# Two-block transformer kernel on one core: the division of the sparse heads' probabilities moved from VectorE to ScalarE, one tile ahead

## The reference, cut to what matters

```
s = jnp.einsum('bqhd,bqkhd->bhqk', qb, k_sel) * (Dh ** -0.5)
s = jnp.where(valid[:, None], s, NEG)
p = jax.nn.softmax(s, axis=-1)          # exp, row sum, division
o = jnp.einsum('bhqk,bqkhd->bqhd', p, v_sel)
```

## Time and profile before

| | before |
|---|---|
| median of 3 runs | 1163.38 us (1163.32 to 1163.65) |
| the profiled execution | 1163.7 us |
| its span, first to last instruction | 1161.6 us |
| PE busy | 1143.0 us (98% of the span) |
| DVE busy | 598.2 us (51%) |
| ACT busy | 288.1 us (25%) |
| POOL busy | 712.4 us (61%) |
| granted TensorE clock, mean | 0.999 |
| sparse tiles, 709 to 777 us: PE / DVE / ACT busy | 65.66 / 49.99 / 41.57 of 68.00 us |

### The profile page before, as it was taken

The page is one execution under the profiler, slowest core; times in us unless marked ns, Lnnn a source line. Parts: engine busy times, 40 slices in busy tenths (PEclk is TensorE's granted clock), DMA queues, the critical chain, the costliest instruction groups (busy, mean ns, idle before and its releaser), DMA issues.

```text
span 1161.6 us, 15385 instructions
## 1 busy us (share of the span) xinstructions
PE 1143.0 (98%) x5319; PEld 923.0 (79%) x5319; DVE 598.2 (51%) x985; ACT 288.1 (25%) x577; POOL 712.4 (61%) x435
## 2 busy tenths in 40 slices
PE   7999999999999999999999998999999999999997
PEld 5888788888888888888777776777888888888886
DVE  4999674540014544448789778846554000455022
ACT  5134362210002111110211346645421000211001
POOL 7879948656666666657456333225876666666662
PEclk9999999999999999999999999999999999999999
DMA  6321224222222222234332221112233223223521
GB/s 243 127 86 60 77 69 143 92 97 103 90 99 99 90 101 99 90 104 133 114 123 92 90 78 57 31 56 73 91 108 108 91 91 109 91 90 108 145 73 73
DMA packets 51394, 113.12 MB, mean 97 GB/s; under 512 B 21520, under 2 KB 22160, under 8 KB 51344
## 3 DMA queue, kind: packets, MB, share of 16 engines
q1 hardware_dynamic: 31200, 105.40, 26.9%
q10 hardware_dynamic: 20144, 7.05, 2.6%
HBM read 102.99 MB, written 2.10 MB: 90 GB/s over the span
## 4 chain that ended last, share of the span: by engine, by line
PE 92%; DVE 6%; issue 1%; ACT 1%; DMA 0%; DVEq 0%; SPq 0%; ACTq 0%
PE bank L561 20%; PE bank L563 20%; PE bank L562 20%; PE bank L1096 5%; PE bank L1098 5%; PE bank L1097 5%; DVE bank L1593 2%; PE bank L941 2%; PE bank L594 1%; PE bank L593 1%; PE bank L595 1%; PE bank L627 1%; PE bank L619 1%; PE bank L620 1%; PE bank L955 1%
## 5 line engine op out<-in xcount | busy, mean ns | idle before, releaser
L426 POOL TENSOR_TENSOR wl<-raw,wh 128x1024 fp32r<-128x1024 f32 x188 | 453.1, 2410 | 15.7
L423 POOL TENSOR_SCALAR wh<-raw 128x1024 fp32r<-128x1024 f32 x188 | 203.4, 1082 | 388.9 <-PE bank L563 231.1
L561 PE MATMUL bank<-xh,wh 128*128 128x512 f32 (+1 forms) x776 | 306.1, 394 | 0.4 <-ACT va L1325 0.4
L562 PE MATMUL bank<-xl,wh 128*128 128x512 f32 (+1 forms) x776 | 300.6, 387 | 0.0
L563 PE MATMUL bank<-xh,wl 128*128 128x512 f32 (+1 forms) x776 | 300.6, 387 | 0.0
L561 PEld LDWEIGHTS bank<-xh,wh 128*128 128x128 f32 x776 | 145.7, 188 | 44.6 <-issue 16.5
L1807 DVE TENSOR_TENSOR ul<-tmb,uh 128x512 f32 x64 | 124.7, 1948 | 90.1 <-ACT uh L1268 90.1
L563 PEld LDWEIGHTS bank<-xh,wl 128*128 128x128 f32 x776 | 145.7, 188 | 29.5
L562 PEld LDWEIGHTS bank<-xl,wh 128*128 128x128 f32 x776 | 145.8, 188 | 27.7 <-issue 0.2
L1267 ACT ACTIVATE tmb<-tmp 128x512 f32<-128x512 f32 x64 | 40.5, 633 | 413.3 <-DVE tmp L1804 413.3
L561 PE MATMUL bank<-uh,wh 128*128 128x512 f32 x288 | 112.6, 391 | 0.0
(11 more groups left out here) (278 smaller groups left out, 1382.0 us busy)
## 6 DMA issues: line engine op xcount, KB each, us to landing
raw<-wstream SPq DMA_DIRECT2D x188, 512.0 KB, 3.2
x<-xT SPq DMA_DIRECT2D x8, 256.0 KB, 4.9
x4r<-x4b ACTq DMA_DIRECT2D x16, 128.0 KB, 2.7
out<-x4r SPq DMA_DIRECT2D x8, 256.0 KB, 2.3
qd<-ropey ACTq DMA_DIRECT2D x16, 64.0 KB, 2.1
kd<-ropey ACTq DMA_DIRECT2D x16, 64.0 KB, 2.0
qa<-ropey SPq DMA_DIRECT2D x16, 64.0 KB, 2.0
ka<-ropey SPq DMA_DIRECT2D x16, 64.0 KB, 2.0
```

The lines of the kernel that those rows point to most:

```text
L423: nc.gpsimd.tensor_scalar(wh[c][:], raw[c][:], 1.0, 1.0, ALU.mult, ALU.mult).then_inc(high_ready, 1)
L426: nc.gpsimd.tensor_tensor(wl[c][:], raw[c][:], wh[c][:].bitcast(F32), ALU.subtract).then_inc(split_ready, 1)
L561: mm(out, wh_, mh, start=start, stop=False)
L562: mm(out, wh_, ml, start=False, stop=False)
```

## The change

`normalise(n)` of a sparse tile keeps only one reciprocal, over the two row sums of the tile together (128x2), and raises a new semaphore `sum_inverted`. It waits for both exponentials of the tile. The two multiplications go to ACT: a new function `divide(n)` waits for `sum_inverted` and scales both halves of the tile in place with `ACT.Copy`. ACT calls it in its step n for tile n + 1, ahead of `exp(n + 2)`, and after `keep_turned(n)`, the roots and the high part of a differential head. Differential tiles stay as they are.

```diff
             def divide(n):
+
+                diff, h, tb = tile_of(n)
+                N = (tb + 1) * P
+                slot = 2 * (n % 3)
+                f = 16 + 4 * (n % 3)
+                act.wait_ge(sum_inverted, n - DIFF_TILES + 1)
+                for e in range(2):
+                    p = probs[slot + e][:, 0:N]
+                    A(p, p, ACT.Copy, scale=soft[:, f + e:f + e + 1]).then_inc(probs_ready, 1)
...
                     A(xh[:, 4 + h], kept[h][:] if h < 2 else NB[:], ACT.Copy).then_inc(xh_ready, 1)
+                if DIFF_TILES <= n + 1 < TILES:
+                    divide(n + 1)
                 if n + 2 < TILES:
                     exp(n + 2)
...
                 else:
-                    for e in range(2):
-                        p = probs[slot + e][:, 0:N]
-                        dve.wait_ge(exp_done, 2 * n + e + 1)
-                        link(V.reciprocal(soft[:, f + e:f + e + 1], soft[:, 8 + slot + e:9 + slot + e]))
-                        V.tensor_scalar(p, p, soft[:, f + e:f + e + 1], None, ALU.mult).then_inc(probs_ready, 1)
+                    dve.wait_ge(exp_done, 2 * n + 2)
+                    V.reciprocal(soft[:, f:f + 2], soft[:, 8 + slot:10 + slot]).then_inc(sum_inverted, 1)
```

More of the change, by code:

```diff
@@ L319, in build @@
             sem("pT_ready"), sem("pv_done"), sem("o_kept"))
-        lam_exp, eps_scaled = sem("lam_exp"), sem("eps_scaled")
+        lam_exp, eps_scaled, sum_inverted = sem("lam_exp"), sem("eps_scaled"), sem("sum_inverted")
         ym_gained, y_scaled, x4_ready, x4_kept = (
@@ L1364, in keep_turned, with divide @@
                     A(pT[n % 2][e][:, 0:N], bank[turn_bank[e]][:, 0:N], ACT.Copy).then_inc(pT_ready, 1)
+            def divide(n):
+                diff, h, tb = tile_of(n)
[6 more added lines that the diff above has]
+                    A(p, p, ACT.Copy, scale=soft[:, f + e:f + e + 1]).then_inc(probs_ready, 1)
             def keep_output(h):
```

## The result

The changed kernel took 1166.51 us (median of 9 runs, 1165.94 to 1169.15) against 1163.38 us (9 runs, 1162.92 to 1166.36): 3.13 us slower, ratio 1.0025 with a 95% interval of 1.0016 to 1.0034. The forecast was 1166.6 us.

A forecast was written before the change was run, and what follows sets the result against it. PE was taken as the bound, so only its waits count. The terms 0.80 + 1.25 + 0.67 + 0.28 + 0.20 = 3.20 us, on a median of 1163.4, gave 1166.6 us; own range 1165.9 to 1167.3, widened to 1165.2 to 1168.4.

The forecast's parts named there:

- Term 1: Steps 16 and 17: division(17) ahead of exp(18) delays ACT's squares, so head_sums(3) starts later on PE: +0.80 us.
- Term 2: Turn(18): division(18) on ACT stands behind the high part, so the turn is later by a further +1.25 us.
- Term 3: Turn(19): division(19) comes only after keep_turned(18) and its copies on ACT, so values(18) starts a further +0.67 us late.
- Term 4: Steps 20 to 26: each division comes 0.7 us or more ahead of its turn, so no added loss: 0.
- Term 5: Step 27: the reciprocal stays behind x3_scale on DVE, and ACT's copies are longer than DVE's: +0.28 us.
- Term 6: Steps 30 and 31: turn(30) gives 0.75 us back, but late division(31) eats that and more: +0.2 us.
- Rival A: Faster: ACT keeps up with all four turns and PE's 2.8 us come back, 1160.6 us; chance 4%.
- Rival B: No change that can be told: turn(30)'s 0.75 us stays, division(31) in time, copies shorter; 1165.3 us; chance 16%.
- Rival C: Clock falls to 1.2 GHz at 725 for 6 us of work, adding 2.7 us: 1169.3 us; chance 12%.
- three signs of being wrong: PE idle under 1 us together at turns 18 and 19; a copy well under 0.6 us; clock below 1.00 between 718 and 732.

The follow-up runs named there:

- second form with matmuls: Changed kernel plus unused dense matmuls: 256 columns ahead of head_sums(3), 512 and 256 ahead of turn(18) and of turn(19); 1166.50 us, ratio 1.0024.
- Tile 30 alone: Kernel before, with ACT dividing only tile 30 and DVE the others; 1162.98 us against 1163.30, ratio 0.9993.
- the two lists: Kernel before, with ACT dividing only tiles 20 to 31 (1163.89 us, ratio 0.9997) or only tiles 16 to 19 (1166.57 us, ratio 1.0025).
- both edits: Kernel before, with step 17's high part moved behind exp(19) and the eight x3_scale put behind DVE's loop; 1162.16 us against 1163.33, ratio 0.9989.
- tile 19 alone: Kernel before, with ACT dividing only tile 19 and DVE the others; 1163.85 us against 1163.22, ratio 1.0009.
- later high part: Kernel before, with the high part of ACT's step 17 moved behind exp(19), DVE dividing all tiles; 1162.99 us against 1163.33, ratio 0.9997.
- narrow matmuls: Unused dense matmuls, 256 to 512 columns, from head_sums(3) on, added to the changed kernel (1166.50 us), later high part (1163.26) and both edits (1161.66).
- wide ones: Changed kernel plus unused dense matmuls: one pair of 512 columns ahead of turn(18), two ahead of turn(19); 1167.29 us, ratio 1.0033.

## Why the prediction was right, step by step

The sign, the size and the mechanism held: ACT has no slack in steps 16 to 18, and what it took on there came out at PE. How close the number came is in part luck (see the sum).

- **Term 1**, the pair of tile 17 ahead of the squares: +0.80 said, +0.79 measured.
- **Term 2**, the pair of tile 18: +1.25 said, 2.06 - 0.79 = +1.27 measured.
- **Term 3**, the pair of tile 19: +0.67 said, 2.83 - 2.06 = +0.77 measured. The 0.1 over is turn(19) at the low clock, 1.41 us: in the second form with matmuls, at full clock, it is 1.27. I had also said that turn(19) would show a wait of 1.8 us; it shows none, since slow work filled it. With no other division on ACT the term is larger, 0.87, so the terms depend on each other and can't be tested one by one and added.
- **Term 4**: 0 said. Turn(23) is 2.8 late as values(18) was, so 0.
- **Term 5**, turn(27): +0.28 said, 3.08 - 2.83 = +0.25 measured.
- **Term 6**, turns 30 and 31: +0.20 said, 3.55 - 3.08 = +0.47 measured. This is the one that was mis-sized, and by its start. From the start of keep_turned(29) to values(30), through division(30), exp(31), the high part, DVE's low part and division(31), I had 776.0 - 769.18 = 6.82 us; it took 775.82 - 768.98 = 6.84. But keep_turned(29) began 0.75 us after turn(29) (768.23), where before it was 0.48:

```profile
765.70 0.60 PE L955 MATMUL bank<-ident,probs 128*128 128x128 f32 x4
```

  That 0.27 is the error of this term. The same delay is 0.75 in the profiles of the three kernels in which ACT divides all 16 tiles, and 0.48 in the other eleven, those with tiles 20 to 31 on ACT among them; why is open. The new wait of 0.57 at L561 is no second error: turn(31) behind it still waits 0.39 for its division, and together they are the idle time of "about 0.9" that I had foretold for turn(31).
- **Sum**: 3.20 said; 3.55 in the stage, the 0.10 of term 3 and the 0.27 of term 6 being nearly all of the difference. It agrees with the median's 3.13 only because 0.4 came back outside the span, which the prediction had left as it was (it took 2.1 us for start and end). Two errors of some 0.4 have cancelled.
- **The copies**: 0.71, 0.61, 0.50 and 0.40 us said; 0.715, 0.615, 0.506 and 0.396 measured, from an operation 60 us away and a step taken from the exponential. The reciprocal of two columns takes 0.158, as one of one column.
- **Rival A** (faster) assumed that ACT would be in time at turn(19). The single pair of tile 19 shows that it isn't even with nothing else in the way.
- **Rival B** (no change) kept the 0.75 of turn(30). Tile 30 alone shows that it is not kept: division(31) comes late, behind ACT's high part and DVE's low part.
- **Rival C** (the clock): the fall came, which I had given 12%, and its price of 2.7 us did not. A clock below 1.00 between 718 and 732 was also one of my three signs of being wrong; I had said that it would stay at 1.00, and on this the prediction was wrong. The price of a matmul came from the earlier trace rows, which I called the low level though the granted clock of that stretch is 1.00 in the profile. The rows at 0.50 bear the factor out all the same: the products of values(17) start every 0.21 us, against 0.11 before. The step that fails there is to charge 6 us of work at half speed as if PE had been the one that others wait for. PE was waiting for ACT in the same microseconds. What a fall costs is a question of who is late: 0.1 us here, 1.49 with tile 30 alone. The Trainium skill (TensorE: Matmul & The Clock Gate, What's actually happening) states that the gate halves the clock by how busy the array has been of late. The 0.50 agrees.

That the first four tiles carry three quarters of the loss is shown by the two lists, and that the low clock carries 0.1 us of it by the second form with matmuls, in one profiled execution. What the time outside the span depends on was only observed: every kernel with the new semaphore has 1.66 to 1.79 us, every one without it 2.05 to 2.20. No run took the semaphore alone.

## What to carry to other kernels

Price a moved operation in the fullest stretch of the engine that takes it, not by that engine's mean (here 61%), and follow each thing that stands behind it in the queue to its consumer: squares, evictions and table loads here, not only the next division. Before you expect a gain from taking one wait away, look for the second one that ends within a tenth of a microsecond of it, such as the eviction of the bank that the same instruction writes. And where an operation is late because another in its queue is blocked, move that one first: taking `x3_scale` out gave 1.2 us, moving the division cost 3.1. Price a fall of the clock by the work of PE that others wait for while it lasts, not by its length.

## What the runs showed of the hardware

- What made the clock fall is open. In the changed kernel it fell to 0.50 at about 719.9, when PE had idled 1.20 us, had done only light work since, and was beginning to idle again. But it also fell in the profiles of four kernels whose waits ahead of turn(18) are before's, 0.41 and 0.18 us or less: to 0.50 (tile 30 alone) and 0.57 (both edits) in 722 to 726, to 0.58 (tile 19 alone) and 0.78 (later high part) in 718 to 722. In four others with these waits, before among them, it stayed at 1.00. With the narrow matmuls, the first of them a step earlier, it stayed at 1.00 in three profiles of three; with the wide ones, which begin only ahead of turn(18), it fell.
- Two DVE operations that start beside POOL's L426 do not end before it, but 0.3 and 0.5 us behind it: 2.38 us for a division that takes 0.49 otherwise (it ends at 754.82, POOL's row at 754.53), and 2.82 for the `x3_scale` of the earlier trace rows (755.44 and 754.90). The first part of the shift (L1992), which reads a PSUM bank, is not held: before, it takes 0.69 us at 716.74 beside an L426 that ends at 717.09, and 0.69 again at 717.36. The Trainium skill (SBUF — State Buffer, Who interferes with whom) states such a lock, and that ACT has its own port. The trace agrees on both: none of the 32 divisions on ACT took more than 0.73 us, and POOL was as busy as before.
- The time outside the span differs by 0.4 us between programs with and without the new semaphore, and no row of the profile shows it.
